# Gate projections of a bidirectional mLSTM block: both operands in two fp32r parts, weight parts side by side as one stationary tile

## The chip, the cores and the metric

The kernel runs on one core of one Trainium2 chip. Times are device microseconds (us) of one launch. The figure that counts is the median of the runs shown; beside it stands one profiled execution, from which all rows of the trace come. ns marks nanoseconds.

## The reference, cut to what matters

Three layers work on x of 1024 tokens by 1024 channels, all in float32: a short convolution with a Fourier mixer, an attention layer, and a second block with a pooling branch and a bidirectional mLSTM. The change touches only the gates of the mLSTM:

```python
c = silu(centred_depthwise_conv_2(u, conv_w, conv_b))
q = headwise(c, w_q)
k = headwise(c, w_k)
v = headwise(u, w_v)
qkv = concatenate([q, k, v], axis=-1)
gates = einsum('bsc,ncg->nbsg', qkv, w_gates) + b_gates[:, None, None, :]
```

u is the part of the input projection that belongs to the mLSTM (1024 channels), and the gates are 16 numbers for each token (two directions, input and forget gate, four heads). q and k are linear in c, and v is linear in u, so the gates are one product of c with 1024x16 weights and one of u with 1024x16 weights.

## The kernel before

Everything is kept with channels on the 128 partitions and the 1024 tokens along them. A projection is cut into **units** of 128 output channels. One unit is 48 matmuls (`unit_tile`, L790): eight blocks of 128 input channels, three products each (high part of the weights by the high and by the low part of the rows, low part of the weights by the high part of the rows, all in fp32r), each in two halves of 512 tokens. GpSimd (POOL) makes the weight parts one unit after the other (`split`, L695 and L697): it begins unit u+2 when unit u is done. The sums go to two PSUM tensors `pair` in turn, which VectorE (DVE) reads.

The input projection of the second block has 32 units. Units 0 to 7 give u. For each of them DVE multiplies the sum by the norm's factor into `u_rows` (`token_scaled`, L2120), then makes the five-tap convolution in `conv_acc` (L2137 and four times L2140); ScalarE (ACT) makes `c_rows` with Silu (L1596). Units 8 to 23 belong to the pooling branch: DVE makes `pooled` (L2156, L2166), TensorE multiplies it by the float32 weights `pw_sb` (L1189, "the mix"), DVE writes `y_d`. Units 24 to 31 give the output gate, beside which DVE and ACT work on rows made of the gates.

`gates(t)` (L1160, L1163) is run by TensorE after unit t+2, for t = 0 to 7. It adds, in PSUM columns of `aux`, the products of the 128x16 weights `gw_eff` with channel block t of `u_rows` and of `c_rows`, in float32: four matmuls of 128x512 for each t, which the profile records as two each. After the last, ACT adds the bias into `gate_rows` (L1603). The order of each engine is the order of the program text; engines meet in semaphores. The weights `gw_eff` come from small matmuls (L1147) in the layer before, copied by DVE.

SyncE's queue (SP) loads the weights three units ahead and stores `gate_rows` to DRAM after the third pooling group (L563); DVE and ACT use them only beside unit 24 and later.

Of the kernel before, what the change touches and what calls it, by code (L numbers as in the profile page):

```python
# [19 lines left out]
P = 128  # L20
S = 1024
D = 1024
KT = D // P
HALF = 512
# [67 lines left out]
def build(nc, x_t, weight_units, channel_params, ident_in, dft_d, dft_s, rope, edge, block_mask,  # L92
          qkv_blocks, gate_w, gate_b, pool_w, reset_mask, out):
    ctx = ExitStack()
    with ctx:
# [45 lines left out]
        def col(name, i=0):  # L141
# [83 lines left out]
        pool_pad = keep("pool_pad", [P, S + 2 * PAD])  # L225
        pooled = keep("pooled", [P, 2, S])
# [3 lines left out]
        pw_sb = keep("pw_sb", [P, 2, 2, MD])  # L230
        gate_rows = keep("gate_rows", [16, S])

# [110 lines left out]
            sem("u_ready"), sem("conv_done"), sem("c_ready"), sem("gate_done"), sem("gate_ready"), sem("gate_stored"))  # L343
        pooled_ready, mix_done, szp_ready = sem("pooled_ready"), sem("mix_done"), sem("szp_ready")
# [27 lines left out]
        def wait_job(eng, job):  # L372

            eng.wait_ge(unit_done, last_unit(job) + 1)

# [387 lines left out]
        def _(pe):  # L763
# [389 lines left out]
            def gates(t):  # L1153
                for half in range(2):
                    cols = slice(half * HALF, (half + 1) * HALF)
                    o = aux[0:16, 2 * HALF + half * HALF:2 * HALF + (half + 1) * HALF]
                    if t == 0:
                        pe.wait_ge(rstd_ready, 4)
                    pe.wait_ge(u_ready, t + 1)
                    pe.matmul(o, gw_eff[:, KT + t, :], u_rows[:, t, 2 + half * HALF:2 + (half + 1) * HALF],  # L1160
                              start=(t == 0), stop=False)
                    pe.wait_ge(c_ready, t + 1)
                    mm = pe.matmul(o, gw_eff[:, t, :], c_rows[:, t, cols], start=False, stop=(t == KT - 1))  # L1163
                if t == KT - 1:
                    mm.then_inc(gate_done, 1)

            for t in range(KT):
                unit(BASE[4] + t, BASE[4] + t, op_hi, op_lo, "in", wait_operand=(t == 0))
                if t == 0:
                    norm_stats(2, acc_g, aux[:, S:2 * S])  # L1170
                    norm_stats(2, acc_c, aux[:, 0:S])
                if t >= 2:
                    gates(t - 2)
            for g in range(4):
                for i in range(4):
                    unit(BASE[4] + 8 + 4 * g + i, BASE[4] + 8 + 4 * g + i, op_hi, op_lo, "in")
                    if g == 0 and i < 2:
                        gates(KT - 2 + i)
# [178 lines left out]
        def _(act):  # L1357
# [239 lines left out]

            for t in range(KT):
                conv_silu(t)
            act.wait_ge(gate_done, 1)  # L1600
# [186 lines left out]
        def _(dve):  # L1787
# [335 lines left out]
            for t in range(KT):  # L2123
                link(dve.memset(u_rows[:, t, 0:2], 0.0))
                link(dve.memset(u_rows[:, t, 2 + S:4 + S], 0.0))
            dve.wait_ge(rstd_ready, 3)
            for t in range(KT):
# [11 lines left out]
                for tap in range(1, TAPS2):  # L2139
                    link(dve.scalar_tensor_tensor(out=acc, in0=u_rows[:, t, tap:tap + S],  # L2140
                                                 scalar=col("conv_w2", TAPS2 * t + tap), in1=acc,
                                                 op0=ALU.mult, op1=ALU.add))
                signal(conv_done)
# [406 lines left out]
```

## Time and profile before

| | us |
|---|---|
| median of 3 runs | 1780.28 (1779.43 to 1780.86) |
| the profiled execution, whole time | 1779.11 |
| its span, from first to last instruction | 1777.3 |
| TensorE matmul busy | 1739.0 (98%) |
| VectorE busy | 1004.7 (57%) |
| ScalarE busy | 622.5 (35%) |
| GpSimd busy | 448.0 (25%) |

The span leaves out 1.81 us of the profiled execution's time. Busy time counts no waits. PE is TensorE's matmuls, PEld its loads of stationary tiles, which lie beside the matmuls.

### The profile page before, as it was taken

The page shows a single profiled execution, that of the slowest core. Times are in us where ns is not written, and L with a number is a line of the kernel's source. Part 1 is how long each engine was busy: PE and PEld are TensorE (multiplying, and loading weights), DVE is VectorE, ACT ScalarE, POOL GpSimd, SP SyncE. Part 2 cuts the span into 40 slices and gives each one's busy share as a digit, 9 for nine tenths or more (in the row PEclk, how much of TensorE's full clock was granted, in tenths as well). Part 3 has the DMA queues.
Part 4 walks back from the last instruction along what each step waited for, and adds up shares of the span by engine and source line. Part 5 has one row for each costly group of instructions (what it writes and reads, how often), then busy time and mean ns, then how long its engine had stood idle before and what let it go on. Part 6 is the DMA issues. An engine that isn't in the chain of part 4 may idle for free.

```text
span 1777.3 us, 21061 instructions
## 1 busy us (share of the span) xinstructions
PE 1739.0 (98%) x8312; PEld 1415.3 (80%) x8312; DVE 1004.7 (57%) x1237; ACT 622.5 (35%) x804; POOL 448.0 (25%) x288
## 2 busy tenths in 40 slices
PE   8999999999999999999999999999999999999997
PEld 6888888887788888887888766777778788788885
DVE  7343326344677777777785665244536367787323
ACT  5110112124556655556611200000023667772002
POOL 4323322333111011010032322222323322214330
PEclk9999999999999999999999999999999999999998
DMA  5122131141000111100522211112113411336112
GB/s 210 36 71 72 48 130 48 48 166 48 25 31 7 36 36 37 36 6 32 202 90 95 83 36 36 48 53 77 61 66 124 143 48 60 119 118 249 48 36 95
DMA packets 40673, 133.69 MB, mean 75 GB/s; under 512 B 5516, under 2 KB 5900, under 8 KB 40320
## 3 DMA queue, kind: packets, MB, share of 16 engines
q1 hardware_dynamic: 40288, 131.83, 20.9%
q8 instruction: 66, 1.08, 0.2%
q10 hardware_dynamic: 288, 0.52, 0.1%
q14 instruction: 31, 0.25, 0.0%
HBM read 100.61 MB, written 31.59 MB: 74 GB/s over the span
## 4 chain that ended last, share of the span: by engine, by line
PE 88%; DVE 8%; ACT 2%; issue 1%; DMA 0%; DVEq 0%; SPq 0%; ACTq 0%
PE pair L790 49%; PE pair L1004 8%; PE pair L1061 5%; PE aux L1034 4%; PE pair L1047 3%; PE aux L1189 2%; PE pair L1296 2%; PE pair L801 1%; PE pair L856 1%; PE aux L790 1%; PE pair L809 1%; DVE stat_b L2016 1%; PE pair L1281 1%; PE pair L1309 1%; PE aux L1309 1%
## 5 line engine op out<-in xcount | busy, mean ns | idle before, releaser
L695 POOL CAST w_hi<-w_raw 128x1024 fp32r<-128x1024 f32 x106 | 116.1, 1095 | 1143.3 <-issue 1134.3
L790 PE MATMUL pair<-op_hi,w_hi 128*128 128x512 f32 x990 | 311.9, 396 | 0.8 <-DVE op_lo L1797 0.8
L790 PE MATMUL pair<-op_lo,w_hi 128*128 128x512 f32 x990 | 305.6, 390 | 0.0
L790 PE MATMUL pair<-op_hi,w_lo 128*128 128x512 f32 x990 | 305.1, 389 | 0.0
L697 POOL TENSOR_TENSOR w_lo<-w_raw,w_hi 128x1024 fp32r<-128x1024 f32 x106 | 267.7, 2525 | 8.5
L790 PEld LDWEIGHTS pair<-op_hi,w_hi 128*128 128x128 f32 x990 | 185.1, 188 | 49.5 <-issue 12.7
L790 PEld LDWEIGHTS pair<-op_lo,w_hi 128*128 128x128 f32 x990 | 186.2, 188 | 39.0
L790 PEld LDWEIGHTS pair<-op_hi,w_lo 128*128 128x128 f32 x990 | 186.1, 188 | 38.9
L1792 DVE TENSOR_TENSOR pt_lo<-pair,pt_hi 128x1024 fp32r<-128x1024 f32 x60 | 73.4, 1224 | 63.5 <-ACT pt_hi L1537 59.9
L1537 ACT ACTIVATE pt_hi<-pair 128x1024 fp32r<-128x1024 f32 x60 | 61.6, 1026 | 122.7 <-issue 84.1
L1004 PE MATMUL pair<-opb_hi,w_hi 128*128 128x512 f32 x256 | 101.1, 395 | 0.6 <-DVEq L86 0.6
L1004 PE MATMUL pair<-opb_hi,w_lo 128*128 128x512 f32 x256 | 99.9, 390 | 0.0
L1004 PE MATMUL pair<-opb_lo,w_hi 128*128 128x512 f32 x256 | 99.7, 389 | 0.0
L1061 PE MATMUL pair<-pt_hi,v_all 128*128 128x256 f32 x480 | 94.3, 289 | 5.0 <-DVE pt_lo L1792 4.4
L1061 PEld LDWEIGHTS pair<-pt_hi,v_all 128*128 128x128 f32 x480 | 77.8, 194 | 15.1 <-DVE pt_lo L1792 13.2
L2016 DVE TENSOR_REDUCE stat_b<-aux 128x1 f32<-128x1024 f32 x64 | 78.4, 1225 | 9.6 <-PE aux L1034 7.4
L1528 ACT ACTIVATE prob<-aux,stat_b 128x1024 f32<-128x1024 f32 x64 | 71.5, 1117 | 10.2 <-DVE stat_b L2017 6.0
L744 POOL TENSOR_TENSOR cq<-c_rows,g_rep 128x256 f32<-128x256 f32 x56 | 43.8, 788 | 122.3 <-PE pair L1296 115.4
L1034 PE MATMUL aux<-k_all,q_hi 128*128 128x512 f32 x256 | 74.0, 411 | 0.0
L1047 PE MATMUL pair<-ident,prob 128*128 128x128 f32 x512 | 66.6, 273 | 2.3 <-DVE prob L2023 1.1
L1061 PE MATMUL pair<-pt_lo,v_all 128*128 128x256 f32 x240 | 68.5, 285 | 0.0
L1607 ACT ACTIVATE sz_p<-sz_p 128x1024 f32<-128x1024 f32 x8 | 8.5, 1057 | 169.6 <-DVE sz_p L2120 169.6
(364 smaller groups left out, 3061.0 us busy)
## 6 DMA issues: line engine op xcount, KB each, us to landing
w_raw<-weight_units SPq DMA_DIRECT2D x106, 512.0 KB, 3.4
xf<-y_dram SPq DMA_DIRECT2D x12, 512.0 KB, 4.7
x_dram<-xa SPq DMA_DIRECT2D x8, 512.0 KB, 5.9
xc<-x_dram SPq DMA_DIRECT2D x8, 512.0 KB, 6.8
x_dram<-xc SPq DMA_DIRECT2D x8, 512.0 KB, 2.9
y_dram<-y_d SPq DMA_DIRECT2D x8, 512.0 KB, 2.7
mz_dram<-y_d SPq DMA_DIRECT2D x8, 512.0 KB, 2.9
bm_b<-bm_dram SPq DMA_DIRECT2D x8, 512.0 KB, 4.7
```

The lines of the kernel that those rows point to most:

```text
L695: pool.tensor_copy(w_hi[:, u % 2, :], w_raw[:, u % 3, :]).then_inc(w_hi_done, 1)
L697: pool.tensor_tensor(w_lo[:, u % 2, :], w_raw[:, u % 3, :], w_hi[:, u % 2, :], ALU.subtract).then_inc(w_split, 1)
L744: pool.tensor_tensor(cq[:, n % 2, d, :, :], c_rows[:, 2 * h:2 * h + 2, cols], g_rep[:, d, cols].unsqueeze(1).broadcast_to([P, 2, P]), ALU. ...
L790: mm = pe.matmul(acc[:, cols], w, x[:, kx, cols], start=(first and k == 0 and n == 0), stop=(last and k == KT - 1 and n == 2))
L1004: mm = pe.matmul(bank, w, x[:, k, cols], start=(k == 0 and n == 0), stop=(k == KT - 1 and n == 2))
L1034: mm = pe.matmul(aux[:, b + half * HALF:b + (half + 1) * HALF], a[:, h % 2, rows], k[:, g, cols], start=(n == 0), stop=(n == 2))
L1047: mm = pe.transpose(pair[0][:, k * P:(k + 1) * P], prob[:, t % 2, k * P:(k + 1) * P], ident[:, :])
L1061: mm = pe.matmul(pair[1][:, HALF:HALF + 2 * P], v[:, g, k, :], p[:, k, :], start=(k == 0 and n == 0), stop=(k == QT - 1 and n == 2))
L1528: link(act.activation(prob[:, t % 2, :], aux[:, (t % 2) * S:(t % 2 + 1) * S], ACT.Exp, bias=stat_b[:, t % 2, 0:1], scale=SCORE_SCALE, accu ...
L1537: link(act.activation(weights_of(m)[0][:, :, (t % 2) * P:(t % 2 + 1) * P], pair[0][:, :].rearrange("p (k q) -> p k q", k=QT), ACT.Copy), p ...
L1792: link(dve.tensor_tensor(lo, full, hi, ALU.subtract), done)
L2016: link(dve.reduce_max(stat_b[:, t % 2, 2:3], aux[:, (t % 2) * S:(t % 2 + 1) * S], AX.X))
```

## The change

Rows and weights of the gates are each written as a high part (rounded to fp32r) and a low part (the rest). The 16 columns of high weights and the 16 of low weights stand side by side in `gw_split`, so that one stationary tile has 32 columns; the high part and the low part of the rows (`gate_parts`) are both multiplied by it and added in 32 rows of PSUM. The product now has a term more than those of the units (low by low). At the end ACT copies the 32 rows to `gate_sums`, and a float32 product with `gate_fold` (two identities of 16 rows one above the other) adds rows 0 to 15 to rows 16 to 31. ACT makes the high parts of the rows (`mixed_hi` of u, `conv_hi` of c), DVE the low parts (`mixed_lo`, `conv_lo`) between the taps of the convolution. The half of `gates` that needs only u is run one unit earlier than before. The new tensors lie where `pooled`, `sz_p`, `y_d` and `gate_rows` are used later, so three waits, for `part_gated` and `gate_done`, are added on DVE in the pooling branch.

```diff
--- before.py
+++ after.py
@@ -223,12 +223,19 @@
         c_rows = keep("c_rows", [P, KT, S])
         conv_acc = keep("conv_acc", [P, 2, S + 2 * PAD])
         pool_pad = keep("pool_pad", [P, S + 2 * PAD])
+        pooled_start = at[0]
         pooled = keep("pooled", [P, 2, S])
         sz_p = keep("sz_p", [P, S])
         y_d_start = at[0]
         y_d = keep("y_d", [P, 2, S])
         pw_sb = keep("pw_sb", [P, 2, 2, MD])
+        gate_rows_start = at[0]
         gate_rows = keep("gate_rows", [16, S])
+
+        gate_parts = nc.alloc_sbuf_tensor_at("gate_parts", [P, 4, S], F32R, offset=pooled_start)
+        gate_sums = nc.alloc_sbuf_tensor_at("gate_sums", [32, S], F32, offset=y_d_start + 4 * S)
+        gw_split = nc.alloc_sbuf_tensor_at("gw_split", [P, 2 * KT, 32], F32R, offset=gate_rows_start)
+        gate_fold = nc.alloc_sbuf_tensor_at("gate_fold", [32, 16], F32, offset=gate_rows_start + 4 * 2 * KT * 32)
 
         at[0] = op_start
         kw_t = keep("kw_t", [P, 2, 2, S])
@@ -341,6 +348,7 @@
         bdt_ready, weff_done, weff_ready = sem("bdt_ready"), sem("weff_done"), sem("weff_ready")
         u_ready, conv_done, c_ready, gate_done, gate_ready, gate_stored = (
             sem("u_ready"), sem("conv_done"), sem("c_ready"), sem("gate_done"), sem("gate_ready"), sem("gate_stored"))
+        part_hi, part_lo, part_gated = sem("part_hi"), sem("part_lo"), sem("part_gated")
         pooled_ready, mix_done, szp_ready = sem("pooled_ready"), sem("mix_done"), sem("szp_ready")
         zp_scaled, mz_scaled = sem("zp_scaled"), sem("mz_scaled")
         pw_loaded = [sem(f"pw_loaded{i}") for i in range(2)]
@@ -372,6 +380,16 @@
         def wait_job(eng, job):
 
             eng.wait_ge(unit_done, last_unit(job) + 1)
+
+        def part_made(t, which):
+
+            return 2 * t + which + 1
+
+        def part_read(t, which):
+
+            if which:
+                return 2 * t + 3 if t < KT - 1 else 2 * KT
+            return max(2 * t, 1)
 
         OP0 = {"even": 0, "y1": KT, "odd": 2 * KT, "y2": 3 * KT, "in": 4 * KT, "y3": 5 * KT}
         UNIT0 = {"even": BASE[0], "y1": BASE[1], "odd": BASE[2], "y2": BASE[3], "in": BASE[4], "y3": BASE[5]}
@@ -1150,32 +1168,54 @@
             pe.wait_ge(weff_ready, 1)
 
 
-            def gates(t):
+            def gate_columns(half):
+
+                return slice(2 * HALF + half * HALF, 2 * HALF + (half + 1) * HALF)
+
+            def gates(t, which):
+
+                if which == 0:
+                    if t == 0:
+                        pe.wait_ge(rstd_ready, 4)
+                        pe.wait_ge(weff_ready, 2)
+                pe.wait_ge(part_lo, part_made(t, which))
                 for half in range(2):
                     cols = slice(half * HALF, (half + 1) * HALF)
-                    o = aux[0:16, 2 * HALF + half * HALF:2 * HALF + (half + 1) * HALF]
-                    if t == 0:
-                        pe.wait_ge(rstd_ready, 4)
-                    pe.wait_ge(u_ready, t + 1)
-                    pe.matmul(o, gw_eff[:, KT + t, :], u_rows[:, t, 2 + half * HALF:2 + (half + 1) * HALF],
-                              start=(t == 0), stop=False)
-                    pe.wait_ge(c_ready, t + 1)
-                    mm = pe.matmul(o, gw_eff[:, t, :], c_rows[:, t, cols], start=False, stop=(t == KT - 1))
-                if t == KT - 1:
-                    mm.then_inc(gate_done, 1)
+                    for part in range(2):
+                        mm = pe.matmul(aux[0:32, gate_columns(half)], gw_split[:, KT * (1 - which) + t, :],
+                                       gate_parts[:, 2 * which + part, cols],
+                                       start=(t == 0 and which == 0 and part == 0),
+                                       stop=(t == KT - 1 and which == 1 and part == 1))
+                mm.then_inc(part_gated, 1)
+
+            def gate_halves():
+
+                pe.wait_ge(part_hi, 2 * KT + 1)
+                for half in range(2):
+                    cols = slice(half * HALF, (half + 1) * HALF)
+                    mm = pe.matmul(aux[0:16, gate_columns(half)], gate_fold[:, :], gate_sums[:, cols],
+                                   start=True, stop=True)
+                mm.then_inc(gate_done, 1)
 
             for t in range(KT):
                 unit(BASE[4] + t, BASE[4] + t, op_hi, op_lo, "in", wait_operand=(t == 0))
                 if t == 0:
                     norm_stats(2, acc_g, aux[:, S:2 * S])
                     norm_stats(2, acc_c, aux[:, 0:S])
+                if t >= 1:
+                    gates(t - 1, 0)
                 if t >= 2:
-                    gates(t - 2)
+                    gates(t - 2, 1)
             for g in range(4):
                 for i in range(4):
                     unit(BASE[4] + 8 + 4 * g + i, BASE[4] + 8 + 4 * g + i, op_hi, op_lo, "in")
-                    if g == 0 and i < 2:
-                        gates(KT - 2 + i)
+                    if g == 0 and i == 0:
+                        gates(KT - 1, 0)
+                        gates(KT - 2, 1)
+                    if g == 0 and i == 1:
+                        gates(KT - 1, 1)
+                    if g == 0 and i == 2:
+                        gate_halves()
                     if i >= 2:
 
                         m = i - 2
@@ -1595,8 +1635,23 @@
                 act.wait_ge(conv_done, t + 1)
                 link(act.activation(c_rows[:, t, :], conv_acc[:, t % 2, 0:S], ACT.Silu), c_ready)
 
+            def mixed_hi(t):
+                act.wait_ge(u_ready, t + 1)
+                if t >= 1:
+                    act.wait_ge(part_gated, part_read(t - 1, 0))
+                link(act.activation(gate_parts[:, 0, :], u_rows[:, t, 2:2 + S], ACT.Copy), part_hi)
+
+            def conv_hi(t):
+                if t >= 1:
+                    act.wait_ge(part_gated, part_read(t - 1, 1))
+                link(act.activation(gate_parts[:, 2, :], c_rows[:, t, :], ACT.Copy), part_hi)
+
             for t in range(KT):
+                mixed_hi(t)
                 conv_silu(t)
+                conv_hi(t)
+            act.wait_ge(part_gated, 2 * KT)
+            link(act.activation(gate_sums[:, :], aux[0:32, 2 * HALF:4 * HALF], ACT.Copy), part_hi)
             act.wait_ge(gate_done, 1)
             act.wait_ge(consts_d, 80)
             act.wait_ge(r_stored, 16)
@@ -2123,6 +2178,22 @@
             for t in range(KT):
                 link(dve.memset(u_rows[:, t, 0:2], 0.0))
                 link(dve.memset(u_rows[:, t, 2 + S:4 + S], 0.0))
+            link(dve.tensor_tensor(gate_fold[:, :], ident[0:32, 0:16], ident[0:32, 16:32], ALU.add))
+            link(dve.tensor_copy(gw_split[:, :, 0:16], gw_eff[:, :, :]))
+            link(dve.tensor_tensor(gw_split[:, :, 16:32], gw_eff[:, :, :], gw_split[:, :, 0:16], ALU.subtract), weff_ready)
+
+            def mixed_lo(t):
+
+                dve.wait_ge(part_hi, part_made(t, 0))
+                link(dve.tensor_tensor(gate_parts[:, 1, :], u_rows[:, t, 2:2 + S], gate_parts[:, 0, :],
+                                       ALU.subtract), part_lo)
+
+            def conv_lo(t):
+
+                dve.wait_ge(part_hi, part_made(t, 1))
+                link(dve.tensor_tensor(gate_parts[:, 3, :], c_rows[:, t, :], gate_parts[:, 2, :],
+                                       ALU.subtract), part_lo)
+
             dve.wait_ge(rstd_ready, 3)
             for t in range(KT):
 
@@ -2140,6 +2211,10 @@
                     link(dve.scalar_tensor_tensor(out=acc, in0=u_rows[:, t, tap:tap + S],
                                                  scalar=col("conv_w2", TAPS2 * t + tap), in1=acc,
                                                  op0=ALU.mult, op1=ALU.add))
+                    if tap == 1 and t >= 1:
+                        conv_lo(t - 1)
+                    if tap == 2:
+                        mixed_lo(t)
                 signal(conv_done)
             dve.wait_ge(c_ready, KT)
             for g, w in enumerate(WINDOWS):
@@ -2163,16 +2238,24 @@
                                          edge_sb[:, g, 1, PAD - right:PAD], ALU.mult))
                     if g >= 1:
                         dve.wait_ge(mix_done, 2 * g)
+                    elif i == 0:
+                        dve.wait_ge(part_gated, part_read(KT - 1, 0))
                     link(dve.scalar_tensor_tensor(out=pooled[:, i, :], in0=total, scalar=1.0 / w,
                                            in1=pool_pad[:, PAD:PAD + S], op0=ALU.mult,
                                            op1=ALU.subtract), pooled_ready)
+                    if n == 0:
+                        conv_lo(KT - 1)
                 for i in range(2):
                     n = 2 * g + i
+                    if n == 0:
+                        dve.wait_ge(part_gated, 2 * KT)
                     token_scaled(BASE[4] + 10 + 4 * g + i, sz_p[:, :], zp_scaled)
                     dve.wait_ge(mix_done, n + 1)
                     dve.wait_ge(szp_ready, n + 1)
                     if n >= 2:
                         dve.wait_ge(y_stored[n % 2], stored("y3", n - 2))
+                    elif n == 1:
+                        dve.wait_ge(gate_done, 1)
                     link(dve.scalar_tensor_tensor(out=y_d[:, n % 2, :], in0=aux[:, 0:S], scalar=col("pool_scale", n),
                                            in1=sz_p[:, :], op0=ALU.mult, op1=ALU.mult), y_made)
```

TensorE's order at the end of unit 4, before the change: the last matmuls of the unit, the four of `gates(2)`, and the first of unit 5 (32x512 or 16x512 is the shape of the result).

```order
L790 MATMUL pair<-op_hi,w_lo 128x512 x2
L1160 MATMUL aux<-u_rows,gw_eff 16x512 [waits u_ready]
L1163 MATMUL aux<-c_rows,gw_eff 16x512 [waits c_ready]
L1160 MATMUL aux<-u_rows,gw_eff 16x512 [waits u_ready]
L1163 MATMUL aux<-c_rows,gw_eff 16x512 [waits c_ready]
L790 MATMUL pair<-op_hi,w_hi 128x512 [waits pair_free1,w_split]
```

The same place of the changed kernel (`unit_tile` is now at L808), where `gates(3, 0)` and `gates(2, 1)` stand.

```order
L808 MATMUL pair<-op_hi,w_lo 128x512 x2
L1185 MATMUL aux<-gate_parts,gw_split 32x512 [waits part_lo]
L1185 MATMUL aux<-gate_parts,gw_split 32x512 x3
L1185 MATMUL aux<-gate_parts,gw_split 32x512 [waits part_lo]
L1185 MATMUL aux<-gate_parts,gw_split 32x512 x3
L808 MATMUL pair<-op_hi,w_hi 128x512 [waits pair_free1,w_split]
```

Four float32 matmuls have become eight in fp32r. There are four of them after unit 1 (where there was nothing), eight after each of units 2 to 8, and four after unit 9.

VectorE's order for one unit t of u, before the change.

```order
L2120 TENSOR_TENSOR u_rows<-pair,acc_g 128x1024 [waits dve_step,unit_done]
L2137 TENSOR_SCALAR conv_acc<-u_rows,par 128x1024 [waits u_ready,c_ready]
L2140 SCALAR_TENSOR_TENSOR conv_acc<-u_rows,par,conv_acc 128x1024 [waits dve_step] x4
L2120 TENSOR_TENSOR u_rows<-pair,acc_g 128x1024 [waits dve_step,unit_done]
```

The same stretch of the changed kernel.

```order
L2175 TENSOR_TENSOR u_rows<-pair,acc_g 128x1024 [waits dve_step,unit_done]
L2208 TENSOR_SCALAR conv_acc<-u_rows,par 128x1024 [waits u_ready,c_ready]
L2211 SCALAR_TENSOR_TENSOR conv_acc<-u_rows,par,conv_acc 128x1024 [waits dve_step]
L2194 TENSOR_TENSOR gate_parts<-c_rows,gate_parts 128x1024 [waits part_hi,dve_step]
L2211 SCALAR_TENSOR_TENSOR conv_acc<-u_rows,par,conv_acc 128x1024 [waits part_lo]
L2188 TENSOR_TENSOR gate_parts<-u_rows,gate_parts 128x1024 [waits part_hi,dve_step]
L2211 SCALAR_TENSOR_TENSOR conv_acc<-u_rows,par,conv_acc 128x1024 [waits part_lo]
```

Two subtractions have come between the taps, and each waits for ACT's copy of the high part.

TensorE's order after unit 10, the first of the units with a mix behind it, in the changed kernel.

```order
L1196 MATMUL aux<-gate_sums,gate_fold 16x512 [waits part_hi]
L1196 MATMUL aux<-gate_sums,gate_fold 16x512
L1229 MATMUL aux<-pooled,pw_sb 128x512 [waits pw_loaded0,pooled_ready]
L1229 MATMUL aux<-pooled,pw_sb 128x512 x3
```

The first two are new; before, the mix followed the unit at once.

## Rows read from the trace of the kernel before

**Rows 1.** The page: busy time by engine, and the granted clock.

```profile
PE 1739.0 (98%) x8312; PEld 1415.3 (80%) x8312; DVE 1004.7 (57%) x1237; ACT 622.5 (35%) x804; POOL 448.0 (25%) x288
...
PEclk9999999999999999999999999999999999999998
```

**Rows 2.** The chain that ended last: start us, length us, engine and line, instructions.

```profile
993.26 21.78 PE pair L790 x96
...
1018.58 11.10 PE pair L790 x48
1029.68 0.96 PE aux L1160 x2
1030.64 0.86 PE aux L1163 x2
1031.50 0.86 PE aux L1160 x2
1032.36 0.86 PE aux L1163 x2
1033.22 11.10 PE pair L790 x48
```

**Rows 3.** The same chain, from the last gate product to unit 30.

```profile
1121.06 11.10 PE pair L790 x48
1132.16 3.43 PE aux L1189 x8
1135.59 10.91 PE pair L790 x48
...
1301.30 65.31 PE pair L790 x288
1366.61 0.61 PE aux L1198 x8
1367.22 11.13 PE pair L790 x48
```

**Rows 4.** Timeline of VectorE, one unit: start us, us, instructions, idle before them.

```profile
1029.72 1.23 DVE L2120 TENSOR_TENSOR u_rows<-pair,acc_g 128x1024 f32<-128x1024 f32 x1 [5.26 <-PE pair L790]
1031.09 2.72 DVE L2137 TENSOR_SCALAR conv_acc<-u_rows,par 128x1024 f32<-128x1024 f32 x1 [0.15 <-DVE u_rows L2120]
1033.85 5.25 DVE L2140 SCALAR_TENSOR_TENSOR conv_acc<-u_rows,par,conv_acc 128x1024 f32<-128x1024 f32 x4
1044.36 1.22 DVE L2120 TENSOR_TENSOR u_rows<-pair,acc_g 128x1024 f32<-128x1024 f32 x1 [5.26 <-PE pair L790]
```

**Rows 5.** Timeline of GpSimd, the same unit.

```profile
1029.81 1.04 POOL L695 CAST w_hi<-w_raw 128x1024 fp32r<-128x1024 f32 x1 [11.18 <-issue]
1030.92 2.34 POOL L697 TENSOR_TENSOR w_lo<-w_raw,w_hi 128x1024 fp32r<-128x1024 f32 x1
```

**Rows 6.** Groups of instructions, 950 to 1250 us, by shape: busy us, mean ns, idle before.

```profile
L2156 DVE TENSOR_TENSOR conv_acc<-pool_pad 128x1039 f32<-128x1039 f32 x6 | 19.4, 3238 | 0.9
L2156 DVE TENSOR_TENSOR conv_acc<-conv_acc 128x1037 f32<-128x1037 f32 x4 | 5.0, 1242 | 0.1
```

**Rows 7.** Timeline of ScalarE beside units 0 to 4.

```profile
996.87 1.06 ACT L1591 ACTIVATE acc_c<-acc_c 128x1024 f32<-128x1024 f32 x1
...
1039.25 1.06 ACT L1596 ACTIVATE c_rows<-conv_acc 128x1024 f32<-128x1024 f32 x1 [13.58 <-DVEq L86]
```

**Rows 8.** Timeline of VectorE, the first unit of u.

```profile
996.93 1.22 DVE L2120 TENSOR_TENSOR u_rows<-pair,acc_g 128x1024 f32<-128x1024 f32 x1 [8.36 <-ACT acc_g L1590]
...
999.42 5.25 DVE L2140 SCALAR_TENSOR_TENSOR conv_acc<-u_rows,par,conv_acc 128x1024 f32<-128x1024 f32 x4
```

**Rows 9.** Loads of stationary tiles, 950 to 1250 us: busy us, mean ns, idle before.

```profile
L790 PEld LDWEIGHTS pair<-op_hi,w_hi 128*128 128x128 f32 x320 | 59.5, 188 | 21.1 <-issue 9.7
L1163 PEld LDWEIGHTS aux<-c_rows,gw_eff 128*16 128x16 f32 x32 | 3.1, 96 | 10.7 <-issue 10.3 <-ACT c_rows L1596 0.3
```

**Rows 10.** SyncE's queue: the store of the gates.

```profile
1252.57 0.43 SPq L563 DMA_DIRECT2D gate_dram<-gate_rows  x1
```

## The prediction

> **What bounds the kernel now.** The page comes first: TensorE is busy for 98% of the span at the full granted clock, the next engine for 57% [rows 1]. So a microsecond is saved only if TensorE's queue becomes shorter by it and nobody else makes it wait. The second view is the chain that ended last. Through the whole place of the change it runs on TensorE without a break: a unit of 48 matmuls, four gate products (eight records), the next unit [rows 2]. Behind the gates it goes on in the same manner [rows 3]. The third view is the timeline of VectorE, the engine that gets new work there: it works for 9.38 us on one unit (1029.72 until 1033.85 + 5.25) and then sits idle for 5.26 us until TensorE has finished the next [rows 4]. One round is 14.64 us.
>
> **What a visit to the gates costs now.** Bare units come from the piece of 288 fp32r matmuls: 65.31 / 288 = 0.2268 us for one, 10.89 us for a unit [rows 3]. A unit that follows gate products takes 11.10 us, 0.21 more. The four products take 0.96 + 3 x 0.86 = 3.54 us, the first of them 0.10 more than the others [rows 2]. A visit is thus 3.75 us, and eight are 30.0 us. The mix is the comparison: also four float32 products of 512 columns, but with full 128-column tiles. It takes 3.43 us and the next unit 10.91 us, so there the 0.31 us around the visit are missing [rows 3]. They go with the change of the tile's shape. Transposes of 32-row tiles (L1198) again leave a unit of 11.13 us behind them [rows 3].
>
> **What a visit costs afterwards.** 64 fp32r matmuls take the place of 32 in float32. The trace has no fp32r matmul with a 32-column tile. Lower bound of its price: a quarter of the float32 product, 0.86 / 4 = 0.215 us. Upper bound: the float32 product itself, 0.86 us. The nearest row is the unit's fp32r matmul with as many moving columns, and I take its 0.2268 us [rows 3]: 64 x 0.2268 = 14.5 us. There are nine visits instead of eight. For each I keep the 0.31 us of today's visits, because 32 columns are again not 128: 9 x 0.31 = 2.8 us. Bounds of that term: nothing, if it belongs to float32 with small tiles, and 0.31 plus an unhidden load for each matmul. A load of a 16-column tile has 0.096 us [rows 9], which would be 64 x 0.096 = 6.1 us more; today it lies beside the product before, whose spacing stays 0.86, so I count none. The product that adds the two groups is two float32 matmuls, 2 x 0.86, and once more 0.31: 2.0 us. Sum afterwards 14.5 + 2.8 + 2.0 = 19.3 us, net **30.0 - 19.3 = 10.7 us less** on TensorE.
>
> A rule that speaks against the change concerns the shape. The row says that a unit behind a small tile is 0.21 us longer and the first small product 0.10 us, and that the full-width mix has neither [rows 2, 3]. The Trainium skill, TensorEngine Tiling (Key Properties), says that changing the tiling mode drains TensorE; the mode of a 32-column tile differs from a full one's. By that rule each of the nine visits and the fold pays, which gives the 10.7 us; without it the gain would be 13.8 us.
>
> [...] By the row the fp32r matmul is 0.2268 us, not a quarter of 0.86 [rows 2, 3]. [...] The trace's own unit is above that, so I stay with the row.
>
> **Work beside it, VectorE.** Each unit of u gets two subtractions of 1024 columns with both inputs in SBUF. The nearest row is 1.24 us (L2156 between `conv_acc` buffers), the dearest of the same kind 3.24 us, when it starts while GpSimd works [rows 6]. Where do the new ones stand? GpSimd ends its two instructions at 1030.92 + 2.34 = 1033.26, and L2137, which began at 1031.09, ends at 1033.81 [rows 4, 5]. The new ones come behind the first and the second tap, 5.4 us and more after the round began, when GpSimd is done. So 1.24 us plus 0.03 each; the round of VectorE becomes 9.38 + 2 x 1.27 = 11.9 us. TensorE's round becomes 10.89 + 0.31 + 8 x 0.2268 = 13.0 us. VectorE still waits, 1.1 us instead of 5.26. Even if it fell behind, TensorE asks for `mixed_lo(t)` only a whole unit after it began: made at 5.4 + 1.3 + 1.3 + 1.3 = 9.3 us of the round, needed at 13.0, 3.7 us of cover. `conv_lo` comes from the round before and is made at 6.7 us. The price of that cover being gone is every microsecond by which the round is longer than 13.0, times seven rounds.
>
> **ScalarE.** It gets 16 copies of about 1.06 us, as its other full-width instructions have [rows 7], and sits idle for 13.58 us of a round now. `conv_hi(t)` must wait until TensorE has run `gates(t-1, 1)`, some 0.31 / 2 + 1.8 = 2.0 us into the round, and `mixed_hi(t+1)` is queued behind it: copies end at about 3.2 and 4.3 us, the subtractions ask at 5.4 and 8.0. Silu of the same unit comes only at 11.9. No cost.
>
> **The first visit is the tight one.** After unit 1 TensorE asks for the low part of block 0. Unit 1 ends at 993.26 + 21.78 / 2 = 1004.15 [rows 2]. On VectorE the first product starts at 996.93 because it waits for the norm, and two taps end at 999.42 + 2 x 1.31 = 1002.05 [rows 8]; ScalarE is free at 997.93 [rows 7], so the high part is there at about 999.3. The low part is ready at 1003.3, 0.85 us early. The weight split (two instructions of 256 columns) goes into the 8.36 us of VectorE's wait [rows 8]. If this cover fails, the loss is a microsecond or so, once.
>
> **The end of the gates.** The sum of the last products is copied by ScalarE beside unit 10, which takes ten times as long. `gate_rows` comes one unit later than before, but its store stands in SP's queue behind the third pooling group, at 1252.57 [rows 10], over 100 us later. VectorE's added waits in the pooling branch are for TensorE's visits after units 8 and 9 and for the fold, all earlier in TensorE's order than the mix for which it waits anyway. After that nothing is new, and since the chain stays on TensorE until unit 30 [rows 3], the saving is not given back by a wait for a fixed moment: weights come three units ahead.
>
> **The sum.** Profiled execution 1779.11 (span 1777.3 and 1.81 around it) - 10.7 = 1768.4. The median lies 1.17 above that execution, so the forecast for it is 1780.28 - 10.7 = **1769.6**.
>
> **The rivals.** (a) *The 0.31 us do not come with fp32r tiles.* For: the rows that show it are float32 products and transposes; against: the mix is float32 too and is free of it [rows 3]. Gain 30.0 - 14.5 - 1.7 = 13.8, with 0.215 us for a matmul 14.5: 1766.5 to 1765.8. (b) *Loads are not hidden.* With so short a matmul there are 0.2268 us to hide one in, against 0.43 today. For: the idle time that the profile puts before loads of 16 columns as waiting for issue; against: 128-column loads of 0.188 us are hidden behind the unit's own matmuls [rows 9]. 10.7 - 6.1 = 4.6 gained: 1775.7. (c) *A 32-column tile runs at float32's rate*, the first rival on the other side: 64 x 0.86 = 55.0 us, with 4.8 for the rest 59.8, against 30.0: 1810. It decides from (30.0 - 4.8) / 64 = 0.39 us per matmul. Nothing in the rows shows the rate depending on the width of the tile: 16 columns and 128 both have 0.86. (d) *VectorE becomes the bound*, also on the other side. If both subtractions cost 3.24 us, as those that begin beside GpSimd [rows 6], the round is 9.38 + 2 x 3.27 = 15.9 us, 2.9 over TensorE's, seven times, less 3.7 of cover: 16.6 lost, 5.9 net: 1786. It decides where the seven rounds and the cover eat 10.7, at a round of 15.1 us. Against: the place behind the taps. (e) *Hardly any gain*: several of these covers fail in part, a round of some 14.5 us; 1778 to 1782.
>
> **How the numbers follow.** Forecast 0.71 (1768 to 1772), (a) 0.13, (b) 0.06, (c) 0.04, (d) 0.03, (e) 0.03. A measurement of this kernel can tell 0.2%, 3.6 us. The forecast, (a) and (b) are faster by more: 0.90; (e) is the same, 0.03; (c) and (d) are slower, 0.07. The range takes in the forecast and (a) with half a microsecond below for the spread of the runs, and reaches upward half way to (b): 1765.2 to 1773.0; what it leaves out is 0.16.
>
> **What the changed profile would show.** Right: in the chain, units 2 to 8 followed by one piece of about 1.9 us of x8 and then a unit of 11.1 us, a round of 13.0 us; VectorE's wait before `u_rows` near 1 us; the subtractions at 1.24 us; two fold products of 0.86 us each before the first mix. Wrong: units of 10.89 behind the gates (a); a spacing of 0.3 us or 0.86 us between the gate matmuls (b, c); TensorE waiting for a `gate_parts` instruction of VectorE (d), or before the first visit near 1004.

## The result

The changed kernel takes 1766.24 us in the median of four runs (1762.46 to 1766.29), the kernel before 1779.86 in the same comparison. The ratio is 0.9915, 95% interval 0.9903 to 0.9928: faster by 0.7 to 1.0%. The forecast was 1769.6 with a range of 1765.2 to 1773.0 and 10.7 us of gain. The median lies inside the range. By the medians 13.6 us were gained. By the ratio the changed kernel stands at 0.9915 x 1779.86 = 1764.7, a gain of 15.1 us, just outside the range. Either way more was gained than forecast.

The changed kernel's page, first part and the granted clock (answers to [rows 1]).

```profile
PE 1726.2 (98%) x8316; PEld 1418.2 (80%) x8316; DVE 1025.7 (58%) x1256; ACT 640.6 (36%) x821; POOL 450.3 (26%) x288
...
PEclk9999999999999999999998999999999999999998
```

TensorE is 12.8 us shorter busy, and the span of the profiled execution is 12.8 us shorter too (1777.3 to 1764.5): TensorE alone was the bound and still is. VectorE and ScalarE have 21 and 18 us more work, of which nothing is seen in the time.

The changed kernel's chain that ended last: start us, length us, engine and line, instructions (answers to [rows 2, 3]; L808 is the units' matmul, L1185 the gate product, L1196 the fold, L1229 the mix).

```profile
993.75 10.90 PE pair L808 x48
1004.66 0.93 PE aux L1185 x4
1005.58 10.89 PE pair L808 x48
1016.48 1.84 PE aux L1185 x8
1018.32 10.91 PE pair L808 x48
...
1105.71 0.92 PE aux L1185 x4
1106.63 10.91 PE pair L808 x48
1117.54 1.81 PE aux L1196 x4
1119.35 3.63 PE aux L1229 x8
...
1137.33 32.67 PE pair L808 x144
```

The reader is to see two things. Eight gate products take 1.84 us, 0.230 each. And the unit behind them takes 10.91 us, where it took 11.10 behind float32 gates: the 0.31 us around a visit are gone. They are still there around the fold, which is float32: it takes 1.81 instead of 2 x 0.86 us, and its successor, the mix, 3.63 instead of 3.43. From the start of unit 1, the first behind the norm's sums, to the start of unit 12, behind the second mix, the chain took 1149.94 - 993.26 = 156.7 us, and now takes 1137.33 - 993.75 = 143.6: **13.1 us less at the place of the change**. What the medians and the ratio show beyond that, 0.5 and 2.0 us, is not seen in this pair of profiles.

The changed kernel's timeline of VectorE, one unit of u (answers to [rows 4]).

```profile
1042.01 1.23 DVE L2175 TENSOR_TENSOR u_rows<-pair,acc_g 128x1024 f32<-128x1024 f32 x1 [0.78 <-PE pair L808]
1043.38 2.79 DVE L2208 TENSOR_SCALAR conv_acc<-u_rows,par 128x1024 f32<-128x1024 f32 x1
1046.21 1.29 DVE L2211 SCALAR_TENSOR_TENSOR conv_acc<-u_rows,par,conv_acc 128x1024 f32<-128x1024 f32 x1
1047.53 1.23 DVE L2194 TENSOR_TENSOR gate_parts<-c_rows,gate_parts 128x1024 fp32r<-128x1024 f32 x1
1048.79 1.28 DVE L2211 SCALAR_TENSOR_TENSOR conv_acc<-u_rows,par,conv_acc 128x1024 f32<-128x1024 f32 x1
1050.11 1.22 DVE L2188 TENSOR_TENSOR gate_parts<-u_rows,gate_parts 128x1024 fp32r<-128x1024 f32 x1
1051.37 2.60 DVE L2211 SCALAR_TENSOR_TENSOR conv_acc<-u_rows,par,conv_acc 128x1024 f32<-128x1024 f32 x2
1054.76 1.22 DVE L2175 TENSOR_TENSOR u_rows<-pair,acc_g 128x1024 f32<-128x1024 f32 x1 [0.79 <-PE pair L808]
```

The subtractions take 1.23 us each, and VectorE waits 0.79 us of a round of 12.75.

### The profile page after: what moved, and what is told of

It reads as the page before. It is cut to its first block, busy times and chain, and to the rows that moved or that the text cites. A ratio compares the mean times of both kernels' runs of the same rounds, so it can differ in the third digit from the quotient of the medians.

```text
span 1764.5 us, 21137 instructions
## 1 busy us (share of the span) xinstructions
PE 1726.2 (98%) x8316; PEld 1418.2 (80%) x8316; DVE 1025.7 (58%) x1256; ACT 640.6 (36%) x821; POOL 450.3 (26%) x288
## 4 chain that ended last, share of the span: by engine, by line
PE 89%; DVE 7%; ACT 2%; issue 1%; DMA 0%; SPq 0%; DVEq 0%; ACTq 0%
PE pair L808 50%; PE pair L1022 8%; PE pair L1079 5%; PE aux L1052 4%; PE pair L1065 3%; PE pair L819 2%; PE pair L1336 2%; PE aux L1229 2%; PE pair L827 1%; PE pair L874 1%; PE aux L808 1%; DVE stat_b L2071 1%; PE pair L1321 1%; PE pair L1349 1%; PE aux L1185 1%
## 5 line engine op out<-in xcount | busy, mean ns | idle before, releaser
L808 PE MATMUL pair<-op_hi,w_hi 128*128 128x512 f32 x990 | 311.2, 396 | 0.2 <-DVE op_lo L1852 0.2
L808 PE MATMUL pair<-op_lo,w_hi 128*128 128x512 f32 x990 | 305.8, 390 | 0.0
L808 PE MATMUL pair<-op_hi,w_lo 128*128 128x512 f32 x990 | 305.7, 390 | 0.0
L808 PEld LDWEIGHTS pair<-op_hi,w_hi 128*128 128x128 f32 x990 | 185.9, 188 | 43.6 <-issue 5.3
L808 PEld LDWEIGHTS pair<-op_hi,w_lo 128*128 128x128 f32 x990 | 186.2, 188 | 38.9
L808 PEld LDWEIGHTS pair<-op_lo,w_hi 128*128 128x128 f32 x990 | 186.2, 188 | 38.9
L1079 PEld LDWEIGHTS pair<-pt_hi,v_all 128*128 128x128 f32 x480 | 76.7, 191 | 15.1 <-DVE pt_lo L1847 13.3
L1065 PEld LDWEIGHTS pair<-ident,prob 128*128 128x128 f32 x512 | 58.5, 140 | 11.2 <-issue 5.7
```

The costliest lines, as they stand in the source:

```text
L808: mm = pe.matmul(acc[:, cols], w, x[:, kx, cols], start=(first and k == 0 and n == 0), stop=(last and k == KT - 1 and n == 2))
L1065: mm = pe.transpose(pair[0][:, k * P:(k + 1) * P], prob[:, t % 2, k * P:(k + 1) * P], ident[:, :])
L1079: mm = pe.matmul(pair[1][:, HALF:HALF + 2 * P], v[:, g, k, :], p[:, k, :], start=(k == 0 and n == 0), stop=(k == QT - 1 and n == 2))
```

## The experiments

### What the switch to a narrow tile costs

Three theories for the 0.31 us: **type** (a tile narrower than 128 columns costs at the switch if it is float32), **width** (16 columns cost in either type, 32 are enough to be free), **mode** (any change of the tile's shape costs, the forecast's reason). The changed kernel's chain already speaks against the last.

The kernel before, with the gate weights in a wider float32 tile filled up with zeros (W = 32, 64, 128; cut, the last two lines stand elsewhere in the kernel, on VectorE):

```diff
-                    pe.matmul(o, gw_eff[:, KT + t, :], u_rows[...], ...)
+                    pe.matmul(o, gw_wide[:, KT + t, :], u_rows[...], ...)   # o = aux[0:W, ...]
+                    link(dve.memset(gw_wide[:, :, 16:W], 0.0))
+                    link(dve.tensor_copy(gw_wide[:, :, 0:16], gw_eff[:, :, :]), weff_ready)
```

W = 32: 

> The kernel before with its 16 gate columns padded by zeros to a 32-column float32 tile. Three theories for the 0.31 us around a visit to the gates, which the kernel before has and the changed one has not. Type: the switch costs where a narrow tile is float32. Then nothing changes here: first product 0.96 us, the other three 0.86, next unit 11.10, time as before within 0.5 us. Width: 16 columns are the cause and 32 are enough to be free. Then four products take 3.43 us, the next unit 10.90, and eight visits give 8 x 0.31 = 2.5 us less. Mode (any change of the tile's shape costs): already against the changed kernel's rows, and it would say as type does.

W = 128: 

> The same with a 128-column float32 tile, as the mix has. Type and width both say that the cost is gone: four products 3.43 us, next unit 10.9, some 2.5 us less than before. If the 0.31 us stay, it is neither the type nor the width but something else of these products, as their waits for u_ready and c_ready between them.

W = 64: 

> The kernel before with its gate weights padded to a 64-column float32 tile. 32 columns still paid at the switch, 128 did not. Either every float32 tile narrower than the array pays (0.97 us for the first product and 11.10 for the next unit, time as before), or the cost ends at half the width (0.86 and 10.89, 3 us less). No theory of mine decides it.

Chain with 32 float32 columns (L1162 and L1165 are the gate products, L791 the units).

```profile
1031.26 0.98 PE aux L1162 x2
1032.24 0.86 PE aux L1165 x2
...
1034.81 11.11 PE pair L791 x48
```

Chain with 64 columns.

```profile
1031.90 1.00 PE aux L1162 x2
1032.90 0.86 PE aux L1165 x2
...
1035.48 11.11 PE pair L791 x48
```

Chain with 128 columns.

```profile
1029.37 0.86 PE aux L1162 x2
1030.22 0.86 PE aux L1165 x2
1031.08 0.86 PE aux L1162 x2
1031.94 0.86 PE aux L1165 x2
1032.80 10.89 PE pair L791 x48
```

With 32 and with 64 columns the first product stays at 0.98 and 1.00 us and the next unit at 11.1; with 128 both are gone. One execution each, in the order 32, 64, 128: 1780.18, 1781.62 and 1776.33 us, beside medians of 1780.3, 1779.4 and 1780.3 for the kernel before. Single executions of the kernel before differ by as much as 5 us (1776.69 to 1781.80), so the chain decides: from unit 1 to unit 12 it takes 156.8, 157.0 and 154.1 us, where the kernel before takes 156.7, so the 128 columns save the expected 8 x 0.31. So in float32 every tile that was tried and is narrower than 128 columns (16, 32, 64) pays some 0.3 us a visit, and a tile eight times as wide as needed is cheaper.

The changed kernel with 16-column fp32r tiles (the low weights are left out, so this is a probe and not the same arithmetic; cut, the copy and the fold take 16 rows instead of 32):

```diff
-                        mm = pe.matmul(aux[0:32, gate_columns(half)], gw_split[:, KT * (1 - which) + t, :],
+                        mm = pe.matmul(aux[0:16, gate_columns(half)], gw_split[:, KT * (1 - which) + t, 0:16],
```

> The changed kernel with 16-column fp32r tiles: only the high parts of the gate weights are used, the low ones are left out of the product. Type: no cost at the switch, eight matmuls 1.84 us, next unit 10.90, time as the changed kernel within 0.5 us. Width: nine visits pay 0.31 us each, eight matmuls some 1.95 us and the next unit 11.1, 2.8 us more than the changed kernel.

Its chain.

```profile
1014.58 1.85 PE aux L1185 x8
1016.44 10.89 PE pair L808 x48
```

Eight products 1.85 us, the unit 10.89: nothing is paid at 16 columns either. It took 1763.95 us in one execution, 2.3 under the changed kernel's median where at most 0.5 was expected, but from unit 1 to unit 12 the chain takes 143.6 us as before. Type stands; width and mode, as causes without the type, fall. Both properties are needed, float32 and fewer than 128 columns. A change of type at the switch is not needed: the mix behind the fold pays its 0.20 us although both are float32. Why a float32 tile that is narrow pays and one that is full does not was not found out.

### What setting the parts side by side is worth

```diff
-                    for part in range(2):
-                        mm = pe.matmul(aux[0:32, ...], gw_split[:, ..., :], gate_parts[:, 2 * which + part, cols], ...)
+                    for n, (side, part) in enumerate(((0, 0), (0, 1), (1, 0))):
+                        mm = pe.matmul(aux[0:16, ...], gw_split[:, ..., 16 * side:16 * side + 16],
+                                       gate_parts[:, 2 * which + part, cols], ...)
-                    if g == 0 and i == 2:
-                        gate_halves()
```

> The part that sets the weight parts side by side is undone: three fp32r products of 16 columns (high by high, high by low, low by high; low by low is left out) and no fold. 96 matmuls instead of 64, 32 x 0.23 = 7.4 us more, and the fold's 2.0 us away. Type: 5.4 us more than the changed kernel, so 1771.6. Width: nine times 0.31 on top, 1774.4. A rival says that 12 matmuls of a visit make TensorE's round long enough to hide something on VectorE; VectorE waits for nothing of that kind, so it changes nothing.

The diff is cut: ScalarE's copy to `gate_sums` and the waits for the fold go too.

Its chain.

```profile
1018.10 2.78 PE aux L1185 x12
1020.88 10.89 PE pair L808 x48
...
1126.14 3.43 PE aux L1228 x8
```

Measured: 1772.22 us (1771.31 to 1772.83), ratio to the kernel before 0.9954 (0.9938 to 0.9971). Against the changed kernel it is 6.0 us more (median against median of another comparison); expected by type were 5.4, by width 8.2. From unit 1 to unit 12 the chain takes 149.0 us, 5.4 more. The matmul takes 0.23 us with 16 columns and with 32, so 16 more columns carry the second product for nothing, and what they cost is the fold, 2.0 us once.

### When VectorE's cover is gone

Each of the 16 subtractions is made twice:

```diff
+                link(dve.tensor_tensor(gate_parts[:, 1, :], u_rows[:, t, 2:2 + S], gate_parts[:, 0, :],
+                                       ALU.subtract))
                 link(dve.tensor_tensor(gate_parts[:, 1, :], u_rows[:, t, 2:2 + S], gate_parts[:, 0, :],
                                        ALU.subtract), part_lo)
```

(and the same in `conv_lo`, cut here).

> The changed kernel with each of the 16 subtractions on VectorE made twice, so that the rule for the lost cover is tried. The changed kernel's rows: VectorE works 11.96 us of a round of 12.75 and waits 0.79. Two more subtractions of 1.26 us make 14.48 us, 1.73 over TensorE's round. The low part of u is then made 11.9 us into the round and asked for at 12.75, 0.85 us of cover. If the rule of the prediction holds (each microsecond over, seven rounds, less the cover): 7 x 1.73 - 0.85 = 11.3 us more, 1777, TensorE waiting for gate_parts of VectorE. If the two PSUM buffers and the order of the gates absorb it after all: 1766. If the doubled subtractions fall beside GpSimd and stretch: above 1780.

Measured: 1783.92 us (1782.49 to 1786.04, ten runs), ratio to the kernel before 1.0027 (1.0018 to 1.0037), 18.9 us over the changed kernel's 1765.06 in the later run described under "Without the fold". 1777 was expected by the rule, above 1780 if the doubled subtractions meet GpSimd. Its waits, 990 to 1120 us, TensorE alone: us, times, longest.

```profile
PE aux L1185 <- DVE gate_parts L2190: 12.5, 5, 6.0
```

Its timeline of VectorE.

```profile
1017.98 1.94 DVE L2188 TENSOR_TENSOR gate_parts<-u_rows,gate_parts 128x1024 fp32r<-128x1024 f32 x1
1019.96 3.25 DVE L2190 TENSOR_TENSOR gate_parts<-u_rows,gate_parts 128x1024 fp32r<-128x1024 f32 x1
...
1063.95 5.28 DVE L2215 SCALAR_TENSOR_TENSOR conv_acc<-u_rows,par,conv_acc 128x1024 f32<-128x1024 f32 x2
1069.38 1.23 DVE L2175 TENSOR_TENSOR u_rows<-pair,acc_g 128x1024 f32<-128x1024 f32 x1
```

Its timeline of GpSimd.

```profile
1017.37 1.48 POOL L713 CAST w_hi<-w_raw 128x1024 fp32r<-128x1024 f32 x1 [8.00 <-issue]
1018.92 3.20 POOL L715 TENSOR_TENSOR w_lo<-w_raw,w_hi 128x1024 fp32r<-128x1024 f32 x1
...
1064.90 3.26 POOL L715 TENSOR_TENSOR w_lo<-w_raw,w_hi 128x1024 fp32r<-128x1024 f32 x1
```

The chain that ended last, where it goes back to TensorE.

```profile
1122.12 1.24 DVE gate_parts L2198
...
1123.40 1.11 PE aux L1185 x4
```

The subtraction that began at 1019.96 ended at 1023.21, 1.09 us after GpSimd's at 1022.12 (alone it takes 1.23), and GpSimd's own takes 3.20 us instead of 2.34 [rows 5]. The Trainium skill, SBUF — State Buffer (SBUF: two separate sides), says that a VectorE instruction with two SBUF inputs and a GpSimd instruction that reads SBUF take a shared pair of ports for the whole of an instruction, the other waiting. The trace agrees: at 1018.92 GpSimd's instruction began while VectorE's of 1017.98 was running and came out longer, and the VectorE instruction behind it then ended one instruction's length after GpSimd's.

So the rule for the lost cover held in kind and was too cheap. From the second unit of u to the first of the pooling branch a round took (1116.76 - 1010.59) / 7 = 15.2 us instead of the 14.48 worked out, because a late VectorE meets GpSimd's work with its subtractions and taps, where before only one instruction of a round did (L2137 in [rows 4]). That makes 5 us. From unit 1 to unit 12 the chain takes 161.4 us, 17.8 more than the changed kernel's 143.6 and 6.5 more than the rule gave. From 997.52 to 1123.36 us it runs almost wholly on VectorE, which waits for no unit of TensorE in that stretch; so VectorE set the pace there. The granted clock fell too in two of the stretches in which TensorE waited (a mean of 0.86 from 1010 to 1035 us and 0.91 from 1080 to 1100, but 1.00 from 1060 to 1080), and since that stretch of the chain lies on VectorE, the low clock there is not what made it longer. The other 1.5 us or so come at the two ends of the rounds, which the rule did not price, and were not taken apart.

### Without the fold

```diff
-                        mm = pe.matmul(aux[0:32, gate_columns(half)], gw_split[...], ...)
+                        mm = pe.matmul(aux[0:48, gate_columns(half)], gw_split[...], ...)   # low weights in columns 32 to 47
-            link(act.activation(gate_sums[:, :], aux[0:32, 2 * HALF:4 * HALF], ACT.Copy), part_hi)
+            link(act.activation(gate_sums[:, :], aux[32:48, 2 * HALF:4 * HALF], ACT.Copy), part_hi)
+                        link(dve.scalar_tensor_tensor(out=gate_rows[:, :], in0=aux[0:16, 2 * HALF:4 * HALF],
+                                                      scalar=gb_sb[:, :], in1=gate_sums[:, :],
+                                                      op0=ALU.add, op1=ALU.add), gate_ready)
```

The diff is cut: the fold's two products, their waits and ScalarE's addition of the bias are gone.

The changed kernel again, for the comparison: 

> The changed kernel once more, beside the three that follow. 1766.2 in most executions; about one in four may be near 1762.5 with a mean granted clock of 0.996 instead of 0.993, as one of its first four was.

Without the fold: 

> The fold product is taken away. The low weight columns stand at columns 32 to 47 of a 48-column tile (columns 16 to 31 are a filling that nobody reads), ScalarE copies PSUM rows 32 to 47 to partitions 0 to 15, and VectorE adds them with the bias. By the changed kernel's rows the fold costs 1.81 us and 0.20 in the mix behind it. If TensorE alone counts: 2.0 us less than the changed kernel, 1764.2. Rival: the new addition on VectorE is on the way to y_d and the mix waits for it; then at most 1.3 us come back. Second rival: a 48-column fp32r tile has the switching cost that 32 columns have not, which would be 9 x 0.31 = 2.8 us and make it 0.8 us slower.

Measured: the changed kernel 1765.06 us (1764.21 to 1765.77, ratio 0.9920, interval 0.9905 to 0.9935; 1766.2 was expected), without the fold 1762.46 (1759.94 to 1764.36, ratio 0.9909, 0.9893 to 0.9926). The intervals overlap, so the times alone do not show a gain; the chain without the fold decides.

```profile
1102.12 0.92 PE aux L1184 x4
1103.04 10.91 PE pair L807 x48
1113.95 3.43 PE aux L1217 x8
```

The fold's 1.81 us and the mix's extra 0.20 are away, and units behind 48-column tiles stay at 10.9. Neither rival shows. From unit 1 to unit 12 the chain takes 141.6 us, 2.0 less than the changed kernel's, as expected; the rest of the 2.6 us between the medians is not seen there.

### The granted clock before the place of the change

In both kernels the clock falls some 80 us before the first gate product, while the 24 small products that make the gates' weights run (L1147 before, L1165 after). In the changed kernel they run from 925.70 to 933.11 us, and the clock is at its lower level from about 928.5 to 938.6; in the kernel before it is there from about 930.5 to 937.3. Busy time and mean granted clock (the number ahead of the last two) of 925 to 935 us, in the kernel before.

```profile
925.00:935.00 10.00, 10.00 (x60) 9.36 (x59) 7.79 (x5) 3.09 (x4) 4.31 (x2) 0.77 0.36 127
```

The same window of the changed kernel.

```profile
925.00:935.00 10.00, 10.00 (x57) 9.50 (x56) 8.62 (x5) 3.03 (x3) 4.32 (x2) 0.67 0.39 131
```

A mean of 0.67 at levels of 2.4 and 1.2 GHz is two thirds of the window at the lower one. Part of the piece itself runs at it. The piece in the changed kernel:

```profile
925.70 7.40 PE aux L1165 x48
```

The same piece in the kernel without the fold, where the clock falls only at about 930.8 and is back at 934.2:

```profile
925.35 5.26 PE aux L1164 x48
```

The experiment puts three of the products behind each block of one unit (all six of the last two blocks behind the seventh):

```diff
-                if e == 3:
-                    for i in range(3 * KT):   # 24 products in one piece
+                unit(BASE[3] + e, BASE[3] + e, opb_hi, opb_lo, "y2", beside=gate_weights if e == 4 else None)
-                if k == 3:
+                if k == 4:
                     dve.wait_ge(weff_done, 1)
```

(Cut: the body of `gate_weights`, and in `unit` its call behind each block.)

> The 24 small products that make the gate weights (128x16 results, L1165, 7.4 us in one piece) are spread over the blocks of one unit, three behind each block. In both kernels' profiles the granted clock falls to about half behind that piece: mean 0.77 (before) and 0.67 (after) between 925 and 935 us, 0.95 and 0.93 up to 960. If that piece is what brings the clock down: clock 1.00 there, mean 0.996, and some 3.8 us less in nearly every execution, 1762.5, the value of the one fast execution. Rival: the fall comes from something else at that place; then the time stays at 1766.2 within a microsecond.

With the edit of e5 as well: 

> Both edits together. They touch different places, so the gains should add: 1766.2 - 2.0 - 3.8 = 1760.4. If only one works, 1764.2 or 1762.5.

The same window with the products spread.

```profile
925.00:935.00 10.00, 10.00 (x57) 8.66 (x57) 8.62 (x5) 3.02 (x3) 4.37 (x2) 1.00 0.39 131
```

Its chain.

```profile
929.65 1.48 PE pair L810 x6
931.13 0.57 PE aux L1167 x6
931.70 1.48 PE pair L810 x6
```

The clock stays at 1.00 there, in the profile of both edits too, while every other profile on record has the fall. Three products take 0.57 us, 0.19 each, and a block of the unit takes 1.48 instead of 1.36 us (10.89 / 8). Spread, the 24 products and the longer blocks are some 5.5 us, no less than the 5.26 of one piece at the full clock, so what is gained is the clock: in the changed kernel the piece takes 7.40 us, 2.1 of them by the lower level, and the units behind it lose the rest. Measured: spread 1761.55 us (1760.62 to 1763.19), ratio 0.9902 (0.9887 to 0.9916); both edits 1760.83 (1760.45 to 1761.06), ratio 0.9896 (0.9881 to 0.9911). That is 3.5 and 4.2 us less than the changed kernel beside them, 3.8 and 5.8 expected. The gains did not add in full between the medians. At the place of the gates they did: from unit 1 to unit 12 both edits take 141.6 us, the spread alone 143.6. The profiled execution of both edits has a second fall of the clock, a mean of 0.97 from 1500 to 1560 us, which the one with the spread alone has not. It belongs to neither edit, for the kernel before and the changed kernel have it too, and the versions with 32 float32 columns, with three products and without the fold have not; whether it is the reason is open. The version with both edits is the fastest measured, 18.9 us under the kernel before.

## Why the prediction was right or wrong

- **TensorE is the bound, and what its queue loses is gained**: right. 13.1 us less at the place, 12.8 in the span.
- **The price of one fp32r matmul with a narrow tile, 0.2268 us by the nearest row**: right to 2%, measured 0.230 (1.84 / 8), 14.7 us for 64. The quarter of a float32 product, 0.215, was the worse guess.
- **The step that failed: "For each I keep the 0.31 us of today's visits, because 32 columns are again not 128: 9 x 0.31 = 2.8 us."** The nine visits pay almost nothing (the unit behind is 10.91 instead of 10.89), some 0.2 us in all. The corrected sum is 14.7 + 0.2 + 2.0 = 16.9 us afterwards, 13.1 net. The mechanism of the gain was right; this term of the sum was too large by 2.6 us, and the price of the matmuls was too small by 0.2. The runs showed in its place that the cost belongs to narrow float32 tiles (16, 32, 64 columns) and to no fp32r tile (16, 32, 48). Rival (a), "the 0.31 us do not come with fp32r tiles", was the case. It stood at 1766.5, beside 1766.24 measured, and had a chance of 0.13. That the median lies in the range is owed to this rival, for whose sake the range reached so low, and not to the sum.
- **Where the evidence was misread**: gates and mix, both float32, differ in width, so width was plainly needed for the cost. Gates and units differ in width and in type, and the forecast never asked whether the type was needed as well. It was. The Trainium skill, TensorEngine Tiling (Key Properties), says that changing the tiling mode drains TensorE, and that made width alone more believable. Measured, a change to a 32-column fp32r tile and back costs next to nothing (10.91 against 10.89 us), so the measurement decides against applying the rule here.
- **The fold**: 2.0 us forecast with 0.31 around it; 1.81 and 0.20 measured, right.
- **VectorE**: round 11.9 forecast, 11.96 measured; TensorE's 13.0 forecast, 12.75 measured, so the wait is 0.79 and not 1.1. No cost, right. The rule for its price if the cover goes, each microsecond over the round times seven less the cover, was too cheap when tried with doubled subtractions: late instructions meet GpSimd, and the loss was 18.9 us between medians, 17.8 in the chain, where the rule gave 11.3. Rival (e) did not follow the rule at all: a round of 14.5 us gives (14.5 - 13.0) x 7 - 3.7 = 6.8 us lost and 1776.4, not 1778 to 1782.
- **ScalarE and the first visit**: right. The high part was made at 998.77 to 999.84, the low part was ready at 1003.77, and TensorE did not wait before the first visit at 1004.66: a cover of 0.9 us, 0.85 forecast.
- **The range**: its lower end took in rival (a) but not what the clock adds. One of the first four executions took 1762.46 us at a mean granted clock of 0.996, the others 1766.2 to 1766.3 at 0.993 or 0.994. The ratio counts that one too. That the clock is what makes the 2.0 us between the ratio's 15.1 and the chain's 13.1 is argued from these mean clocks and not shown. The range had no room for such a spread because the three times shown of the kernel before lay within 1.4 us.

## What to carry to other kernels

When a cost sits at the border between two kinds of instruction, list every property in which they differ (type, width, rows) and give each a number before charging it to the new kind: here that one choice was the whole error. In place of a float32 product with few output channels, two fp32r parts of the weights side by side in one tile, run over two parts of the rows, take about half the time (1.84 against 3.44 us a visit) and no switch, for a fold of 2.0 us once; if float32 must stay, a tile filled up with zeros to 128 columns is cheaper than a narrow one, by 0.31 us a visit. Cover on an engine that shares ports with another is not linear: once it is late, its instructions meet others than before.

## What was not expected of the hardware

- The switch between full-width fp32r products and narrow float32 ones costs 0.10, 0.12 and 0.14 us on the way in at 16, 32 and 64 columns, 0.21 on the way back at each of them, and nothing at 128.
- Small products in one piece (24 of 128x16 results, 5.26 us at the full clock) bring the granted clock to its lower level though TensorE never stops: before the piece ends, or just behind it, and for 3 to 10 us, by an amount that differs from execution to execution (mean 0.67, 0.77 and 0.83 from 925 to 935 us in three profiles). Spread over a unit they leave it at 1.00, 3.5 us less in the median, though they and the blocks between them take no less in sum (some 5.5 us more than the bare unit) than one piece at the full clock.
- The number of columns of an fp32r tile does not show in the product's time: 16, 32 and 48 columns all give 0.23 us, while the load grows from 94 to 108 and 121 ns beside it.
